# Hybrid encoder trunk in fp32: first weight half on another queue, a cast moved, sums by column halves, another slot for the last w_down half

## What is computed

```python
for l in range(DEPTH):
    h = rms_norm(x, pre_mix_gain[l])
    proj = h @ w_in[l]                      # q | k | v | u
    ya = window_attention(q, k, v, attn_sinks[l])
    yp = multiscale_pool(u, pool_w[l], pool_scale[l])
    y = jnp.concatenate([rms_norm(ya, attn_out_gain[l]), rms_norm(yp, pool_out_gain[l])], axis=-1)
    x = x + rms_norm(y @ w_out[l], post_mix_gain[l])
    h = rms_norm(x, pre_ffn_gain[l])
    f_out = swiglu(h, ...) if l % 2 == 0 else moe_swiglu(h, ...)
    x = x + rms_norm(f_out, post_ffn_gain[l])
```

## Time and profile before

| | |
|---|---|
| median of three runs | 1143.63 us |
| the profiled execution's own time | 1147.92 us |
| its span, first to last instruction | 1146.1 us |
| mean granted TensorE clock | 0.992 |
| TensorE matmuls busy | 1123.8 us, 98% |
| VectorE busy | 891.5 us, 78% |
| ScalarE busy | 758.1 us, 66% |
| last chain, by engine | PE 87%, DVE 7%, ACT 3%, DMA 2% |

### The profile page before, as it was taken

One profiled execution on the slowest core, in us unless ns is written; L12 is line 12 of the kernel. 1 busy time (PEld: TensorE's weight loads), 2 busy tenths in 40 slices (PEclk: granted clock), 3 DMA queues, 4 the chain that ended last, 5 costly groups with the idle time before them and its releaser, 6 DMA issues.

```text
span 1146.1 us, 14128 instructions
## 1 busy us (share of the span) xinstructions
PE 1123.8 (98%) x5479; PEld 935.0 (82%) x5479; DVE 891.5 (78%) x791; ACT 758.1 (66%) x788; POOL 49.3 (4%) x74
## 2 busy tenths in 40 slices
PE   7999999998999999999999999999999999999996
PEld 7988888887998878888888888888888888888884
DVE  5567444445668799888889888889888898888896
ACT  6666433444665667777777777777777777777764
POOL 3000000000000001001001000100100100000200
PEclk8999999999999999999999999999999999999998
DMA  8747655551447799999999999999999999999992
GB/s 250 247 156 246 197 181 183 183 179 48 169 142 263 275 354 369 383 391 366 381 382 369 386 377 379 383 368 395 365 389 377 367 377 384 376 370 367 398 336 76
DMA packets 174531, 349.11 MB, mean 305 GB/s; under 512 B 9288, under 2 KB 58480, under 8 KB 174464
## 3 DMA queue, kind: packets, MB, share of 16 engines
q1 hardware_dynamic: 169824, 332.17, 80.3%
q0 software_dynamic: 4448, 15.77, 3.8%
q10 hardware_dynamic: 192, 0.27, 0.1%
HBM read 342.41 MB, written 5.77 MB: 304 GB/s over the span
## 4 chain that ended last, share of the span: by engine, by line
PE 87%; DVE 7%; ACT 3%; DMA 2%; issue 1%; SPq 0%; ACTq 0%; DVEq 0%
PE ps L1296 27%; PE ps L1298 27%; PE ps L1297 27%; DVE lo_gu L2282 2%; PE ps L1722 1%; DMA raw_gu<-in_moe_w_up 1%; PE ps L1432 1%; DVE lo_d L2289 1%; ACT hi_gu L1139 1%; PE ps L1765 1%; DMA raw_gu<-in_w_in 1%; ACT xt_hi L904 1%; DVE lo_gu L1879 1%; PE ps L1303 0%; PE ps L1423 0%
## 5 line engine op out<-in xcount | busy, mean ns | idle before, releaser
L2282 DVE TENSOR_TENSOR lo_gu<-raw_gu,hi_gu 128x2048 fp32r<-128x2048 f32 x176 | 395.8, 2288 | 58.3 <-ACT hi_gu L1139 58.2
L1296 PE MATMUL ps<-hi_gu,xt_hi 128*128 128x512 f32 (+1 forms) x1056 | 410.0, 388 | 4.5 <-DVE lo_gu L1895 2.1
L1298 PE MATMUL ps<-hi_gu,xt_lo 128*128 128x512 f32 (+1 forms) x1056 | 403.7, 382 | 0.0
L1297 PE MATMUL ps<-lo_gu,xt_hi 128*128 128x512 f32 (+1 forms) x1056 | 402.6, 381 | 0.0
L1139 ACT CAST hi_gu<-raw_gu 128x2048 fp32r<-128x2048 f32 x176 | 327.8, 1909 | 2.6 <-DMA raw_gu<-in_moe_w_up 2.4
L1149 ACT CAST hi_d<-raw_d 128x1024 fp32r<-128x1024 f32 x172 | 172.1, 1049 | 137.9 <-PE ps L1298 136.1
L1296 PEld LDWEIGHTS ps<-hi_gu,xt_hi 128*128 128x128 f32 x1056 | 199.9, 189 | 42.8 <-issue 3.8
L1298 PEld LDWEIGHTS ps<-hi_gu,xt_lo 128*128 128x128 f32 x1056 | 199.6, 189 | 39.1
L1297 PEld LDWEIGHTS ps<-lo_gu,xt_hi 128*128 128x128 f32 x1056 | 200.1, 189 | 36.7
L2289 DVE TENSOR_TENSOR lo_d<-raw_d,hi_d 128x1024 fp32r<-128x1024 f32 x172 | 202.7, 1220 | 21.8 <-ACT hi_d L1149 21.8
L1296 PE MATMUL ps<-hi_d,ht_hi 128*128 128x512 f32 x424 | 169.3, 399 | 0.7 <-DVE lo_d L2289 0.5
(11 more groups left out here) (266 smaller groups left out, 823.5 us busy)
## 6 DMA issues: line engine op xcount, KB each, us to landing
raw_gu<-in_moe_w_gate SPq DMA_DIRECT2D x176, 512.0 KB, 6.0
raw_gu<-in_moe_w_up SPq DMA_DIRECT2D x176, 512.0 KB, 7.5
raw_d<-in_moe_w_down SPq DMA_DIRECT2D x88, 1024.0 KB, 8.0
raw_gu<-in_dense_w_gate SPq DMA_DIRECT2D x22, 512.0 KB, 4.0
raw_gu<-in_dense_w_up SPq DMA_DIRECT2D x22, 512.0 KB, 5.0
raw_d<-in_dense_w_down SPq DMA_DIRECT2D x11, 1024.0 KB, 5.0
raw_gu<-in_w_out SPq DMA_DIRECT2D x16, 512.0 KB, 8.3
raw_gu<-in_w_in SPq DMA_DIRECT2D x14, 512.0 KB, 6.5
```

The source lines that it names most:

```text
L1296: pe.matmul(o, a_hi, b_hi, start=first, stop=False)
L1297: pe.matmul(o, a_hi, b_lo, start=False, stop=False)
L1298: return pe.matmul(o, a_lo, b_hi, start=False, stop=last)
L2282: dve.tensor_tensor(flat_piece(lo_gu, slot_at), flat_piece(raw_gu, slot_at), flat_piece(hi_gu, slot_at).bitcast(F32), ALU.subtract).then_i ...
```

## The change

Seven things are edited.

- The transfer of KV's first half (512 KB) leaves SyncE's queue and is ScalarE's first, ahead of the two of the gain rows.
- In layer 0's start ScalarE and VectorE take each half of KV's weights ahead of the tokens' part of the same half, and Q0 ahead of the sums of squares of both tiles. `turn_gains` now stands between the fourth and the fifth transpose of tile 0, and `warm` runs 4 and 4 times in place of 6 and 5.
- `split_first(2)` stands ahead of `post_mix(1)` on ScalarE and of `scale_of` and `post_halves` on VectorE. TensorE turns tile 1 at the third step of chunk 1 in place of the first.
- `scaled_sum` works by two column halves, with `x_half_updated` after the first and `x_updated` after the second; `turn_raw` waits for the first before its first transpose and for the second before its fifth.
- The second w_down half of the last chunk is split into the first two k rows of the slot in `hi_gu` and `lo_gu` that the last gate and up weights held (`last_down`). Its cast waits for `gu_used`; in exchange the casts of layer 1's Q0 and Q1, which share that slot, wait for `d_used`.
- In layer 1 TensorE runs two dummy matmuls ahead of `turn_raw` and three behind it (`keep_busy`).
- A tensor `room` of 384 bytes per partition is allocated behind `gain_cols` (96 bytes) and `half_sums` (32 bytes), and is not used.

```diff
--- before.py
+++ after.py
@@ -186,6 +186,8 @@
+
+        room = sb("room", [P, 96])
@@ -303,6 +305,10 @@
+        def last_down(ring):
+
+            return ring[:, (use_ffn(0) + NCH - 1) % 2, 0:2, :].rearrange("p k c -> p (k c)")
+
@@ -363,6 +369,7 @@
         x_updated = sem("x_updated")
+        x_half_updated = sem("x_half_updated")
@@ -549,9 +556,10 @@
-                    sp.dma_start(raw_gu[:, slot, 0:KT // 2, to],
-                                 w[0:KT // 2 * P, c0:c0 + n].rearrange("(k p) n -> p k n", p=P)
-                                 ).then_inc(first_loaded[m], 16)
+                    if m == M_U0:
+                        sp.dma_start(raw_gu[:, slot, 0:KT // 2, to],
+                                     w[0:KT // 2 * P, c0:c0 + n].rearrange("(k p) n -> p k n", p=P)
+                                     ).then_inc(first_loaded[m], 16)
                     k0, kn = KT // 2, KT // 2
@@ -823,6 +831,9 @@
         def _(act):
+            act.dma_start(raw_gu[:, mix_piece(0, M_KV)[0], 0:KT // 2, 0:FC],
+                          w_in[0][0:KT // 2 * P, HALF:HALF + FC].rearrange("(k p) n -> p k n", p=P)
+                          ).then_inc(first_loaded[M_KV], 16)
             act.dma_start(gain_rows[0:2 * KT, :], pre_mix_gain.rearrange("l (k p) -> (l k) p", p=P)
@@ -850,7 +861,7 @@
                 if m in (M_Q0, M_Q1) and l:
-                    act.wait_ge(gu_used, NCH)
+                    act.wait_ge(d_used, NCH)
                 elif m in (M_U1A, M_U1B):
@@ -987,17 +998,17 @@
                     act.activation(spare[:, 1:2], eps[:, 0:1], ACT.Sqrt)
+                    split_half(M_KV, 0)
                     raw_high(l, T_MIX, 0, 0)
-                    split_half(M_KV, 0)
+                    split_half(M_KV, 1)
                     raw_high(l, T_MIX, 0, 1)
-                    split_half(M_KV, 1)
-                    pre_mix(l, 0)
                     raw_high(l, T_MIX, 1, 0)
...
                     split_half(M_U0, 1)
+                    split_mix(l, M_Q0)
+                    pre_mix(l, 0)
                     pre_mix(l, 1)
-                    split_mix(l, M_Q0)
                     split_mix(l, M_Q1)
@@ -1045,8 +1056,8 @@
                     split_first(l, 1)
+                    split_first(l, 2)
                     post_mix(l, 1)
-                    split_first(l, 2)
                     split_first(l, 3)
@@ -1120,8 +1131,9 @@
                     for k in range(2):
-                        act.wait_ge(*((d_half_used, 1) if k == 0 else (d_used, chunk)))
-                        act.copy(hi_d[:, k, :], raw_d[:, chunk % 2, k, :]).then_inc(d_hi_done, 1)
+                        act.wait_ge(*((d_half_used, 1) if k == 0 else (gu_used, NCH)))
+                        act.copy(hi_d[:, 0, :] if k == 0 else last_down(hi_gu), raw_d[:, chunk % 2, k, :]
+                                 ).then_inc(d_hi_done, 1)
                         if k == 0:
@@ -1310,20 +1322,30 @@
+            def keep_busy(times):
+
+                some = ht_hi_end[:].rearrange("p k s -> p (k s)")
+                for _ in range(times):
+                    pe.matmul(ps[:, B_WARM, :], some[:, 0:P], some, start=True, stop=True)
+
...
-            def turn_raw(l, n, t):
+            def turn_raw(l, n, t, between=None):
...
                 if not first:
-                    pe.wait_ge(x_updated, TT * (2 * l - (n == T_MIX)) + t + 1)
+                    pe.wait_ge(x_half_updated, raw_id(l, n, t) - 1)
                 elif t:
...
                 for k in range(KT):
+                    if between and k == KT // 2:
+                        between()
+                    if not first and k == KT // 2:
+                        pe.wait_ge(x_updated, TT * (2 * l - (n == T_MIX)) + t + 1)
                     if first and t == 0 and k % 4 == 0:
@@ -1477,15 +1499,16 @@
                     pe.wait_ge(zeros_warm, 1)
-                    warm(6)
-                    turn_gains()
-                    turn_raw(l, T_MIX, 0)
-                    warm(5)
+                    warm(4)
+                    turn_raw(l, T_MIX, 0, turn_gains)
+                    warm(4)
                     kv(l, 0, lambda: turn_raw(l, T_MIX, 1))
...
                 else:
+                    keep_busy(2)
                     turn_raw(l, T_MIX, 0)
+                    keep_busy(3)
                     kv(l, 0)
@@ -1620,7 +1643,7 @@
                             before_second()
-                        if isinstance(chunk, int) and (chunk, t, k) == (1, 0, 0):
+                        if isinstance(chunk, int) and (chunk, t, k) == (1, 0, 2):
                             turn_raw(0, T_FFN, 1)
@@ -1652,8 +1675,11 @@
                             cols = slice(n * 512, (n + 1) * 512)
-                            last = mm3(ps[:, B_Y + 2 * t + n, :], hi[:, k, a], lo[:, k, a],
-                                       hi_d[:, k, cols], lo_d[:, k, cols], c == 0 and k == 0, ended and k == 1)
+                            w_hi, w_lo = hi_d[:, k, cols], lo_d[:, k, cols]
+                            if ended and k:
+                                w_hi, w_lo = last_down(hi_gu)[:, cols], last_down(lo_gu)[:, cols]
+                            last = mm3(ps[:, B_Y + 2 * t + n, :], hi[:, k, a], lo[:, k, a], w_hi, w_lo,
+                                       c == 0 and k == 0, ended and k == 1)
                         if ended and (t, k) == (0, 1):
@@ -1954,8 +1980,10 @@
                 r = scale_of(norm_id(l, n, t))
-                dve.scalar_tensor_tensor(x_res[:, t, :], rows[:, t, :], r, x_res[:, t, :], ALU.mult, ALU.add
-                                         ).then_inc(x_updated, 1)
+                for h in range(2):
+                    cols = slice(h * HALF, (h + 1) * HALF)
+                    dve.scalar_tensor_tensor(x_res[:, t, cols], rows[:, t, cols], r, x_res[:, t, cols], ALU.mult, ALU.add
+                                             ).then_inc((x_half_updated, x_updated)[h], 1)
@@ -2046,17 +2074,17 @@
                 if l == 0:
+                    split_half(M_KV, 0)
                     raw_low(l, T_MIX, 0, 0)
-                    split_half(M_KV, 0)
+                    split_half(M_KV, 1)
                     raw_low(l, T_MIX, 0, 1)
-                    split_half(M_KV, 1)
-                    scale_of(norm_id(l, PRE_MIX, 0))
                     raw_low(l, T_MIX, 1, 0)
...
                     split_half(M_U0, 1)
+                    split_mix(l, M_Q0)
+                    scale_of(norm_id(l, PRE_MIX, 0))
                     scale_of(norm_id(l, PRE_MIX, 1))
-                    split_mix(l, M_Q0)
                     split_mix(l, M_Q1)
@@ -2141,8 +2169,10 @@
                         dve.wait_ge(d_hi_done, chunk * 2 + (k + 1))
-                        dve.tensor_tensor(lo_d[:, k, :], raw_d[:, c % 2, k, :], hi_d[:, k, :].bitcast(F32), ALU.subtract
-                                          ).then_inc(d_lo_done, 1)
+                        hi, lo = hi_d[:, k, :], lo_d[:, k, :]
+                        if k and c == NCH - 1:
+                            hi, lo = last_down(hi_gu), last_down(lo_gu)
+                        dve.tensor_tensor(lo, raw_d[:, c % 2, k, :], hi.bitcast(F32), ALU.subtract).then_inc(d_lo_done, 1)
...
                     dve.wait_ge(ht_hi_done, chunk + 1)
```

## The result

The changed kernel takes 1135.62 us (median of four runs, 1135.46 to 1136.64) against 1143.54 us of the kernel before on the same chip (four runs, 1142.97 to 1146.58): ratio 0.9927, 95% interval 0.9909 to 0.9946, faster by 8 us. The forecast was 1137.5. The time lies inside the range, near its lower end, but for another reason than the prediction's: 5 to 7 us of it come from the 384 bytes of room, for which the prediction took nothing, and what it did count gives some 3.4 us and not 6.1.

What follows compares the result with a forecast made beforehand. TensorE, busy throughout the expert stage, bounds the kernel, so gains come from its waits and low-clock stretches elsewhere. 2.6 + 1.4 - 1.0 + 1.0 + 0.55 + 1.5 = 6.05, say 6.1; 1143.63 - 6.1 = 1137.5 us, range 1135.2 to 1142.2.

Steps and rivals of the forecast that it cites:

- part 1: Kernel start: KV's first half lands at 6.2, first matmul at 9.0, Q0's low part done 2.6 us earlier.
- part 2: Clock in q: with 1.3 to 1.4 us of idle left it stays up, 1.4 us gained, chance about 0.7.
- part 3: Dense network's start: the 0.57 us wait goes, but the third tile waits for hidden(0); costs 1.0 us.
- part 4: Last w_down half: its cast comes 1.65 us earlier and TensorE's wait goes; gains 1.0 us.
- part 5: x_res by column halves at layer 1's start: TensorE's first four transposes start earlier; gains 0.55 us.
- part 6: Clock in layer 1: less idle and dummy matmuls prevent the fall at 280.8; gains 1.5 us, chance 0.9.
- part 7: 384 bytes of room shift the tensors allocated behind: nothing taken, 3.1 us as bound to both sides.
- nothing is later for them: Kernel start: gain rows coming at 6.5 are copied by 7.1, before ScalarE's first cast ends at 7.25; no delay.
- fewer dummy matmuls cost nothing: Kernel start: 8 dummies in place of 11 cost nothing, as they stood where TensorE waited.
- the bound that I named: Kernel start: Q0 lands by 16.5, just in time for 16.8; it is what would be late next.
- The thin cover of U1's low part: Before q's second half: U1's low parts done at 33.2 against 33.4, 0.2 us to spare; otherwise some tenths lost.
- rival (d): Slower through shifted tensors: from 4.1% on 1032 expert-stage matmuls the kernel is over 0.3% slower; chance 0.03.

Runs made afterwards that it cites:

- part 3 undone: Changed kernel with split_first(2) again behind post_mix(1) and tile 1 turned at the first step of chunk 1: 1135.12 us, ratio to before 0.9909.
- part 4 undone: Changed kernel with the last w_down half in hi_d again, its cast behind d_used; only profiled, layer 1's first transpose at 273.41 against 272.21.
- part 5 undone: Changed kernel with x_res updated in one operation and the transposes waiting for all of it; only profiled, layer 1's first transpose 0.85 us later.
- the last kernel above: Changed kernel with 192 bytes of room, part 3 undone, and gain rows issued by SyncE behind x's tile 0: 1132.29 us, ratio to before 0.9885.
- the start alone: Kernel before with only the new start (KV half on ScalarE's queue, new cast order, gain columns between transposes, fewer dummies): 1143.0 us, ratio 0.9979.
- the queue alone: Kernel before with only the first KV weight half issued first on ScalarE's queue; only profiled, span 1144.0 us, q at 24.26.
- the room alone: Kernel before with only the unused 384-byte tensor added: 1138.04 us against 1145.93, ratio 0.9938.

## Why the prediction was right and wrong

Against the kernel without the room the steps can be measured one by one, by the difference of the starts of the same instruction in two profiled executions. These are single executions, and the one of the kernel before is a slow one of its kind (see the second error below).

| step | predicted, us | measured, us |
|---|---|---|
| part 1, start to q | +2.6 | +2.26 (23.62 to 21.36); 3.18 in the changed kernel |
| part 2, clock in q | +1.4 | +1.48 (k_rows turned at 31.17 and 27.43, less 2.26) |
| part 3, dense start | -1.0 | -1.13 with the halves (3.49 ahead before it, 2.36 behind); -0.8 alone (part 3 undone) |
| part 4, last w_down half | +1.0 | +1.14 (part 4 undone) |
| part 5, column halves | +0.55 | +0.41 (part 5 undone) |
| part 6, clock in layer 1 | +1.5 | +1.45 (3.95 ahead at 278.27, 5.4 behind at 285.75); the fall is in 1 of 8 executions with the old waits |
| sum | 6.05 | 5.7 in the span (1146.1 to 1140.4) |
| part 7, room | 0 | 5.1 in the two networks; 6.5 in the span (1140.4 to 1133.9), of which 0.9 stand before q (21.36 to 20.44) |

**Part 1** came out near its sum, but not by the steps that it named. The half landed at 5.1, not at 6.2. Stretches of time of the kernel before, for the first transfers:

```profile
3.20:5.20 2.00, 2.00 (x7) 1.15 (x6) 0.18 (x1) 0.19 (x1) 1.82 (x10) 1.00 0.69 175
```

and of the changed one:

```profile
3.20:5.20 2.00, 1.53 (x6) 0.83 (x4) 0.00 (x0) 0.84 (x3) 1.82 (x10) 1.00 1.06 368
```

The DMA engines were at 0.69 and 175 GB/s while one queue held everything but the small gain rows, and at 1.06 and 368 GB/s with two. One pair of executions overstates it. In the six kernels with the old start the half landed at 6.56 to 7.98 (7.4 in the mean) with 175 to 278 GB/s in this stretch; in the eleven that issue it first at 0.83 on ScalarE's queue it landed at 5.12 to 5.60 (5.3) with 334 to 379 GB/s. The Trainium skill (DMA: Bandwidth & Descriptors, section "Issuing engines are not separate DMA queues") has several issuing engines save only issue time; from the 7.98 of before that made 7.06, and from the mean of 7.4 it makes 6.5. The traces don't agree: 5.3, and 2.1 to 2.2 MB moved by 8 us in place of 1.7 to 2.0. A part of it is order, not rate: the half no longer stands behind x's second half, which landed at 4.1 to 4.4 before and at 5.8 to 6.4 now. No run separates the two. The gain rows landed when I said, about 6.5, but "nothing is later for them" was wrong, since it stood on a first cast that would end at 7.25; it ended at 6.19. And "fewer dummy matmuls cost nothing" was wrong: behind the 1.88 us of idle the four dummies took 2.05 us (1.17 in the last kernel above) and the first KV matmuls are 0.21 us apart, the pace of the low level in the earlier trace rows, while the column of the granted clock reads 1.00. That the smaller number of dummies did this is not shown. No other number of the changed kernel's start is as unsteady: over the kernels with this start and the weights ahead of the gain rows q begins between 19.78 and 21.36. Q0's landing at 16.1 is the bound that I named (16.5), and it is what holds q once the gain rows don't.

The thin cover of U1's low part cost 0.25 us: the lead of 3.74 us at 27.43 is 3.49 when x_res is turned (79.79 and 76.30).

**Parts 2 and 6** have the right size for one fall, and the clock stayed up in the changed kernel; but they took each fall as certain in the kernel before, and that is wrong. Before q, nine profiled executions have an idle of 1.65 to 2.37 us, and the clock fell in five of them (not with 256 bytes of room, nor in the start alone, the queue alone and the last kernel above); in the eight with 0.58 to 1.24 us it fell in none. So a shorter wait goes with fewer falls there, and part 2 is worth its 1.5 us in a part of the executions. At the turn to layer 1, eight executions have the old waits of about 0.9, 0.9 and 1.24 us, and the clock fell in one, the kernel before's. That the change keeps the clock up there is not shown, and that the dummies were needed is not either: without them it stayed up too.

**Part 3** was right in mechanism and size: the wait for hidden (1.1 said, 0.80 seen) takes the place of the wait of 0.57, of which 0.17 is left. **Parts 4 and 5** were right. The second place of part 5, at the dense network's start, stands inside part 3's sum, which was reckoned with the halves at 94.3 and 94.9; that the halves cost 0.3 us there in the old order (23.4 against 23.1 above) had not been said.

**The step that failed is part 7.** "I take nothing" rested on one pair of mean durations in the earlier trace rows, 400 and 397 ns, taken as the whole effect of place and operand. The other two forms of the same view say 395 against 390 and 395 against 391, and durations of overlapping matmuls aren't the pace: from start to start the trace of before has 0.2335 us for w_down and 0.2284 for gate and up. That is 5.1 ns on each of 1272 w_down matmuls (3 x 424 in the page's groups), 6.5 us, and it was there to be read. What the new place gave is 0.2335 - 0.2292 = 4.3 ns each, 5.5 us, against 5.1 and 6.3 us found in the two networks by the two pairs of kernels with and without the room; in the dense network alone, 240 times 4.3 ns is 1.0 us, and 0.98 was measured. The bound of 3.1 us stood only in rival (d), only as a loss, with a chance of 0.03; the same mechanism on the other side had no chance at all. With it as a gain of up to 6.5 us, the forecast of 1137.5 would have had 1131 as its lower side.

**A second error hid the first.** The sum was made against the profiled execution, which had three stretches at 0.50, and then taken in full from the median. The executions of before run from 1142.67 us (clock 0.996) to 1147.79 (0.992), so a kernel that removes the falls gains 2.9 us less against the first than the table says. The start is unsteady as well: in the six kernels that have the old one q begins at 21.28 to 23.62, 22.5 in the mean, with the profiled execution of before the latest; in nine with the new one at 19.78 to 21.36, 20.5 in the mean. As an estimate from these counts, part 1 is worth 2.0 us, part 2 five sixths of 1.48 (the clock fell in q in five of the six), part 6 an eighth of 1.45, and with -1.13, -0.25 for U1, 1.14 and 0.41 that makes 3.6 us. The median of the kernel without the room says 0.9970, or 3.4 us, where the profiled pair has 5.7 and the prediction 6.1. So that the forecast of 1137.5 is only 1.9 us off is luck: 2.7 us too much in parts 1 to 6 stand against 5 to 7 us left out in part 7. 3.4 and the 7.1 of the room alone are more than the 7.9 found in the first set of runs; the medians of before differ by 2.4 us between the two sets (1143.54 and 1145.93), and no more can be said.

## What to carry to other kernels

Where an engine is the bound, read its pace from start to start for each kind of its instructions before asking which waits go: a difference of 2% between two kinds of the same shape (0.2335 and 0.2284 us) is worth more here than all the waits that were moved (5 to 7 us against 3.4). Whoever adds or removes a tensor moves all that is allocated behind it, so look where the operands that TensorE loads begin, and try 128 bytes behind a multiple of 256. That place is the best of the six tried in this kernel; no other kernel was tried. A gain from stretches at the low clock is had only in those executions that fall; count it against the median at the share of executions that show it, and look at more than one execution of the kernel before, for the one profiled may be its slowest.

## What the runs showed that was not expected

- Place: w_down matmuls run at 0.2273 us from start to start with ht_hi and ht_lo 128 bytes behind a multiple of 256, 0.2292 at 64, and 0.2329 to 0.2335 at 0 and 192. The room moves every tensor behind it (silu, hidden, y_sb too), so that it is the operands loaded by TensorE is argued from whose pace changes (the w_down matmuls by 4 to 6 ns, gate and up by under 1 ns), not shown: ht_hi and ht_lo alone were not moved.
- A 512 KB transfer issued first on a second queue at 0.83 us landed after 4.3 us; the same one issued at 1.89 us, behind two small ones, after 8.8 us (8.1 in a second kernel); in SyncE's queue at 1.75, after 6.2 us (4.8 to 6.2 in six kernels). Why the order of two small transfers costs so much is open.
- The pace of TensorE fell to 0.21 us per 256 columns from 7.6 to about 10.8 us in the changed kernel while the granted clock read 1.00.
- The same waits, to within 0.05 us, were followed by a fall of the clock in one execution of eight at the turn to layer 1.
- An operation of 1024 columns on VectorE took 1.28 us in one and 1.42 us in two halves.
